# Attention probabilities reordered by key blocks before they go through HBM, and a new order of ScalarE's work in a stop

## The reference, cut to what matters

```python
for i in range(DEPTH):                      # DEPTH = 2, 1024 tokens, 1024 features, float32
    z = rmsnorm(h, norm1[i]) @ w_in[i]      # pool input, q, k, v
    ...
    attn_out = dilated_mixer(q, k, v)       # 12 heads of 64, three patterns (dilation 1, 4, 16)
    h = h + concat([pool_out, attn_out]) @ w_out[i]
    h = h + square(relu(rmsnorm(h, norm2[i]) @ w_up[i])) @ w_down[i]
    gate = sigmoid(rmsnorm(h, norm3[i]) @ w_gate[i])
    h = h + gate * (p[i] @ w_ple[i])
...                                         # then one hybrid layer of another kind

# dilated_window_attention, for one block of 128 queries of one head:
s = q_block @ keys_of_this_and_previous_block.T * 64 ** -0.5   # masked
e = exp(s - max(s))
o = (e / sum(e)) @ v                        # the kernel divides later, by shares of the patterns
```

## Time and profile before

| | |
|---|---|
| median of 3 runs | 3103.16 us (3102.33 to 3103.45) |
| the profiled execution | 3097.3 us, its span 3095.6 us |
| PE busy | 3005.9 us, 97% of the span |
| DVE, POOL, ACT busy | 2117.8, 1947.8, 1029.4 us |
| mean granted TensorE clock | 0.988 |

### The profile page before, as it was taken

The page is one execution under the profiler, slowest core; times in us unless marked ns, Lnnn a source line. Parts: engine busy times, 40 slices in busy tenths (PEclk is TensorE's granted clock), DMA queues, the critical chain, the costliest instruction groups (busy, mean ns, idle before and its releaser), DMA issues.

```text
span 3095.6 us, 39370 instructions
## 1 busy us (share of the span) xinstructions
PE 3005.9 (97%) x14012; PEld 2422.1 (78%) x14012; DVE 2117.8 (68%) x2868; ACT 1029.4 (33%) x1879; POOL 1947.8 (63%) x1630
## 2 busy tenths in 40 slices
PE   8899799999999999898999999999999999999999
PEld 7677588888888888666788888888888777788887
DVE  6666485556888965565485557888868988797223
ACT  4122144333444420221253334444331344402102
POOL 6632257887999646432358888999546544476575
PEclk9999899999999999999999999999999999999999
DMA  5666424446444322657334446554211100111112
GB/s 165 144 142 150 122 86 152 154 154 246 152 150 158 93 89 78 146 125 186 71 108 156 153 150 246 157 151 161 58 46 48 35 28 28 30 43 55 45 57 87
DMA packets 605969, 356.21 MB, mean 115 GB/s; under 512 B 300624, under 2 KB 534096, under 8 KB 604240
## 3 DMA queue, kind: packets, MB, share of 16 engines
q1 hardware_dynamic: 333216, 222.34, 23.7%
q10 hardware_dynamic: 272560, 131.37, 15.2%
HBM read 250.55 MB, written 99.94 MB: 113 GB/s over the span
## 4 chain that ended last, share of the span: by engine, by line
PE 82%; DVE 5%; DMA 4%; ACTq 4%; ACT 2%; issue 2%; SPq 0%; DVEq 0%
PE ring L1588 11%; PE ring L1590 11%; PE ring L1589 11%; PE ring L1834 4%; PE ring L1833 4%; PE ring L1832 4%; PE ring L1866 4%; PE ring L1865 4%; PE ring L1867 4%; ACTq L2260 3%; PE aux L1588 3%; PE aux L1590 3%; PE aux L1589 3%; DMA probs_scratch<-probs 3%; PE aux L1832 2%
## 5 line engine op out<-in xcount | busy, mean ns | idle before, releaser
L1295 POOL TENSOR_TENSOR w_hi<-w_raw,ones_r 128x512 fp32r<-128x512 f32 (+3 forms) x296 | 331.1, 1119 | 646.0 <-PE ring L1590 572.4
L1298 POOL TENSOR_TENSOR w_lo<-w_raw,w_hi 128x512 fp32r<-128x512 f32 (+3 forms) x296 | 376.8, 1273 | 23.2
L1588 PE MATMUL ring<-Q_hi,w_hi 128*128 128x512 f32 x752 | 300.3, 399 | 1.7 <-DVE Q_lo L2711 1.7
L1590 PE MATMUL ring<-Q_hi,w_lo 128*128 128x512 f32 x752 | 293.3, 390 | 0.0
L1589 PE MATMUL ring<-Q_lo,w_hi 128*128 128x512 f32 x752 | 293.0, 390 | 0.0
L1588 PE MATMUL ring<-P_hi,w_hi 128*128 128x512 f32 x656 | 268.3, 409 | 3.1 <-DVE v_feat L2784 1.8
L1589 PE MATMUL ring<-P_lo,w_hi 128*128 128x512 f32 x656 | 257.3, 392 | 0.0
L1590 PE MATMUL ring<-P_hi,w_lo 128*128 128x512 f32 x656 | 257.0, 392 | 0.0
L3215 DVE SCALAR_TENSOR_TENSOR conv_out<-conv_in,taps,conv_out 128x1021 f32<-128x1021 f32 (+29 forms) x120 | 187.9, 1613 | 0.2
L1588 PEld LDWEIGHTS ring<-Q_hi,w_hi 128*128 128x128 f32 x752 | 141.1, 188 | 56.4 <-issue 26.3
L1590 PEld LDWEIGHTS ring<-Q_hi,w_lo 128*128 128x128 f32 x752 | 141.2, 188 | 30.1
(11 more groups left out here) (488 smaller groups left out, 8496.3 us busy)
## 6 DMA issues: line engine op xcount, KB each, us to landing
hid_scratch<-stages SPq DMA_DIRECT2D x196, 256.0 KB, 2.1
w_raw<-in_w_in SPq DMA_DIRECT2D x84, 512.0 KB, 3.9
w_raw<-in_w_down SPq DMA_DIRECT2D x64, 512.0 KB, 3.6
p_slot<-hid_scratch ACTq DMA_DIRECT2D x50, 512.0 KB, 4.7
q_slot<-hid_scratch ACTq DMA_DIRECT2D x48, 512.0 KB, 4.7
probs_scratch<-probs ACTq DMA_DIRECT2D x40, 512.0 KB, 3.2
probs_t<-probs_scratch ACTq DMA_DIRECT2D x160, 128.0 KB, 3.0
w_raw<-in_w_up SPq DMA_DIRECT2D x36, 512.0 KB, 4.6
```

Source lines behind the costliest of these rows:

```text
L1295: g.tensor_tensor(w_hi[:, slot, ks], w_raw[:, slot, ks], one.broadcast_to([P, width, P]), ALU.mult).then_inc(w_hi_ready, 1)
L1298: g.tensor_tensor(w_lo[:, slot, ks], w_raw[:, slot, ks], w_hi[:, slot, ks].bitcast(F32), ALU.subtract).then_inc(w_ready, 1)
L1588: t.matmul(o, wh, xh, start=first, stop=False)
L1590: return t.matmul(o, wl, xh, start=False, stop=last)
```

## The change

`probs` is laid out by key groups first, so that what one load wants of a partition's row is one run of 256 numbers (1 KB). DVE's transposes write into that layout and `attend` reads from the same one, in runs of 32 numbers 1 KB apart. ACT's order in a stop becomes: loads of `fetch_probs`, exponentials, and `take_attended` last. `fetch_v` moves from ahead of the unit's first stop to behind its first `send_probs`. And `turn_p` and `take_p` of the second half of the tokens move behind the last `lower_h` and `raise_h`. In the diff below the loops of `fetch_probs` and `exp_block` in `attention_stop`, which stay as they are, are left out, and of `LATE` only DVE's side is shown; ACT's is alike.

```diff
-    probs = place("probs", [P, 2, 2, 256], at=at_Q + 14 * TILE)
+    probs = place("probs", [P, SQUARES, 2, 2, 2, 32], at=at_Q + 14 * TILE)
-    probs_t = place("probs_t", [P, 2, 2, 256], at=at_ple + 1024)
+    probs_t = place("probs_t", [P, SQUARES, 2, 2, 2, 32], at=at_ple + 1024)
...
                 mm = t.matmul(attend_bank[rows, cols], v_t[buf][:, jj, rows],
-                              probs_t[:, half, e, at + b * P:at + b * P + P], start=(b == 0), stop=(b == len(blocks) - 1))
+                              probs_t[:, :, half, e, at // P + b], start=(b == 0), stop=(b == len(blocks) - 1))
...
         def fetch_probs(l, unit, i):
             no = stops_before(l, unit, i)
             act.wait_ge(probs_sent, 16 * (no + 1))
             act.wait_ge(attended, step_no(l, unit, blocks_of(unit, i)[0]))
-            squares = probs_d[no % 2].rearrange("(a t) (x b j) -> b t x a j", a=SQUARES, b=SQUARES, j=32)
+            squares = probs_d[no % 2].rearrange("(a t) (b w) -> b t a w", a=SQUARES, b=SQUARES)
             for b in range(SQUARES):
-                to = probs_t[32 * b:32 * b + 32].rearrange("t x e k -> t (x e k)").rearrange("t (x a j) -> t x a j", a=SQUARES, j=32)
-                act.dma_start(to, squares[b]).then_inc(probs_back, 16)
+                act.dma_start(probs_t[32 * b:32 * b + 32].rearrange("t a x e k j -> t a (x e k j)"), squares[b]).then_inc(probs_back, 16)

         def attention_stop(l, parts):
-            for unit, i in parts:
-                if i >= 2:
-                    for j in blocks_of(unit, i - 2):
-                        take_attended(l, unit, j)
...
+            for unit, i in parts:
+                if i >= 2:
+                    for j in blocks_of(unit, i - 2):
+                        take_attended(l, unit, j)
...
                 elif kind == "step":
-                    if args[1] == 0:
-                        fetch_v(l, args[0])
                     attention_stop(l, unit_parts(*args))
                 elif kind == "send":
                     send_probs(l, *args)
+                    if args[1] == 0:
+                        fetch_v(l, args[0])
...
             for x in range(2):
-                mm = v.transpose(probs[:, x].rearrange("q e k -> q (e k)"), turned[x])
+                mm = v.transpose(probs[:, :, x].rearrange("q b e k j -> q (e k) b j"), turned[x].rearrange("q (n b j) -> q n b j", b=SQUARES, j=32))
...
-            if i in LATE:
+            if i in LATE and LATE[i][1] == 0:
                 turn_p(l, *LATE[i])
...
             lower_h(l, HN3_ORDER[-1:])
+            for c in range(2):
+                turn_p(l, c, 1)
```

More of the change, by code:

```diff
@@ L2249, in send_probs @@
             act.wait_ge(probs_turned, step_no(l, unit, blocks_of(unit, i)[-1]) + 1)
-            act.dma_start(probs_d[no % 2], probs[:].rearrange("q x e k -> q (x e k)")).then_inc(probs_sent, 16)
+            act.dma_start(probs_d[no % 2], probs[:].rearrange("q b x e k j -> q (b x e k j)")).then_inc(probs_sent, 16)
         def fetch_probs(l, unit, i):
@@ L2501, in _ @@
             for i in range(2 * UP - 1, 4 * UP):
-                if i in LATE:
-                    c, hf = LATE[i]
-                    woven(l, late_at(1 + 2 * hf, c))
+                if i in LATE and LATE[i][1] == 0:
+                    woven(l, late_at(1, LATE[i][0]))
                 raise_h(l, [HN3_ORDER[i]])
+            for c in range(2):
+                woven(l, late_at(3, c))
             for f in range(KC):
```

## The result

| | before | changed |
|---|---|---|
| median, runs on the same chip | 3102.74 us (4 runs, 3095.70 to 3103.45) | 3060.09 us (4 runs, 3056.16 to 3061.96) |
| ratio, 95% interval | 1 | 0.9866 (0.9848 to 0.9883) |
| the profiled execution | 3097.3 us | 3061.96 us, its span 3060.2 us |

The change makes the kernel 1.3% faster: some 41 us, where 61 had been worked out. The time lies in the range, 18 us above the forecast, but outside the 3028 to 3056 that the forecast mechanism was given for itself.

A forecast was written before the change was run, and what follows sets the result against it. PE, busy 97% of the span, bounds the kernel; waits of 23.4 + 20.3 + 1.7 = 45.4 us plus 16 of clock make 61.4 off 3097.3, 3035.9, and 5.9 to the median gives 3042 us; range 3018 to 3080.

The forecast's parts named there:

- the forecast mechanism: Attention of both layers: 45.4 us of PE idle and 16 of clock return, 3042 us; own range 3028 to 3056, chance 0.54.
- The issue by the lower bound: ACT's four probability loads per stop: issue of 706 ns a load nears 377 ns, gaining 1.3 us a stop.
- rival D: DVE's transposes and PE's attend: strided operands double both, 3086 us, with DVE's part perhaps 3095 to 3105; chance 0.05.
- the first term of the sum: PE's 39.7 us of waits for probability loads: 2 stay at layers' first loads, 14.3 in the tail, 23.4 go.
- the tail: Late attention stops: six waits for probabilities, 14.3 us, counted as kept; shorter issue's gain is taken by the copies' new wait.
- the crowded stop: Near 307 us, DMA engines busy: four issues of 11.6 us should come near 2.8; PE waits 13.1 us there.
- the question that the prediction left open: Crowded stop's 11.6 us of issue: up to 8.8 stays once a layer, or goes if small pieces each wait for large.
- The waits at new units: PE's waits at a unit's first stop, 6.3 us in one: moving fetch_v behind the first send_probs should end them.
- A: Attention: only new-unit waits go, the crowded stop's 13.1 us stay, clock returns 10 at most; 37 us gained, 3066; chance 0.24.
- B: Attention: more comes back, the tail loosens by 14 us and the clock returns 25; 84 us gained, 3019; chance 0.10.
- C: Every attention stop: attend waits for ACT's moved copies; at 2.5 us beyond the limit 3142 us, slower; chance 0.05.
- E: Attention: no change in time, if ACT's lateness is merely passed on to DVE's order; chance 0.02.

The follow-up runs named there:

- the reversal in both directions: Copies (take_attended) moved last alone on the kernel before: 3096.70 us, 0.9993; copies put back first on the changed kernel: 3063.39 us, 0.9890.
- the second profile of the changed kernel: The changed kernel measured once more with nothing altered: 3062.29 us, 0.9876 against the kernel before.
- the two mends together: Changed kernel with unit 3's fetch_v moved behind take_rows and the hx reloads spread over three panels: 3048.52 us, 0.9855 against the kernel before.

## Why the prediction was right or wrong

**What held.** The place: nearly all of the gain lies in the attention. The packets, to within 10. The issue by the lower bound: 706 to 453 ns, 1.0 us a stop where 1.3 was taken (the bound was 377 ns a load). The 20.3 us of `v_feat` and the 1.7 of `Q_lo` went. The clock gave back some 13 us for 16. Strided transposes and operands cost nothing: 716 ns for 717, and one matmul of `attend` has a median of 273 ns in both kernels. With that rival D is out. The quiet landing, 3.0 us, did not move.

**The step that failed** is the first term of the sum, "39.7 - 2 - 14.3 = 23.4 us go". The waits of `attend` fell by 8.1 us, to 31.6. By place, from the timeline (0.3 us are in stalls too small for it):

| | before | said to stay | measured |
|---|---|---|---|
| first load of a layer | 3.5 | 2 | 5.6 (2.02 and 3.58) |
| the other stops of units 0 to 4 | 21.9 | 0 | 5.6 (0.51; and behind a moved `fetch_v` 0.54, 2.63 and 1.96) |
| the tail, its stops in the crowd | 5.4 (0.27, 1.75 and 3.42) | 5.4 | 13.4 (4.50, 1.44 and 7.50) |
| the tail, the last two attends of a layer | 8.8 (4.21, 1.46 and 3.17) | 8.8 | 6.7 (1.29, 2.03, 1.80 and 1.57) |

The last two rows are the 14.3 us that were kept. Of the second layer's crowd before, two stalls:

```profile
1458.90 0.79 PE L1588 MATMUL ring<-pool_hi,w_hi 128*128 128x512 f32 x1 [5.43 <-DVE v_feat L2784]
...
1478.67 1.60 PE L1656 MATMUL aux<-probs_t,v_t 128*64 128x128 f32 x12 [3.42 <-DMA probs_t<-probs_scratch]
```

Three things were read wrongly in it.

*The crowd has more than one end.* The prediction took the crowded stop to be a matter of issue, and the issue did shrink: 11.56 us became 1.84 with the DMA engines as full as before. But the landings stayed long. The loads issued at 308 landed after 6.2 to 9.7 us (5.4 to 11.5 before), which is the wait of 4.50 us in the first layer. And `fetch_probs` begins only when the store has landed, and that store has 4 KB rows already; nothing in the change helps it. What the DMA engines did while it was under way, in the changed kernel from 1426 to 1442 us: the busy share in slices, and the issues.

```profile
DMA  9999999999999999999999999999999999679951
...
DMA packets 3805, 5.10 MB, mean 319 GB/s; under 512 B 1271, under 2 KB 2788, under 8 KB 3804
...
hx<-h_scratch SPq DMA_DIRECT2D x3, 512.0 KB, 12.4
probs_scratch<-probs ACTq DMA_DIRECT2D x1, 512.0 KB, 15.9
```

Six reloads of 512 KB are issued at 1424.5 on the other queue, the store at 1426.2. So what left under the name of `v_feat` came back in part under that of `attend`: at the two crowded places PE waited 13.1 + 5.4 us for `v_feat` and 5.4 for `attend`, 23.9 in all, and waits 13.4 now. That the reloads are the cause is borne out by the run that spreads them: no store took over 8.8 us in it.

For the question that the prediction left open: of the 11.56 us of crowded issue, up to 8.8 might have stayed; 1.84 us in all is measured, and 2.24 right behind the reloads with the pieces alone, so nearly all of it went with the number of pieces. The rule that the prediction cites from the Trainium skill (DMA: Bandwidth & Descriptors, "Queues, rings and completion order"), that a DMA engine changes between rings after a packet of descriptors, was taken there to keep the issue long; that was not so here. A store of 4 KB rows could still be slow to issue in the crowd (3.25 us with the pieces alone), and its landing was slow. What the engines did from piece to piece is not in the trace.

*A moved instruction stands in front of others.* `fetch_v` was held against the landing of the store and counted at 0 to 0.3 us. Behind the store its four issues take 3.3 to 6.3 us (889 ns a load at the median, for 705), not 2.95, so the cover of some 3 us is short; the first load of a layer is one that pays for it (5.6 us for 3.5). And the queue it was moved into was read only up to `fetch_probs`: for unit 3, `take_rows` comes next. That wait rose by 7.3 us, and putting it right brought it back to 5.3.

*The credit went to the wrong part.* The waits at new units were to end by moving `fetch_v`. The move alone gives 5 us; the pieces alone give all 41, and with them the new-unit wait at 142 fell from 6.3 to 1.7 us though `fetch_v` stays where it was. A microsecond less of issue in the stops before lets ScalarE come to the new unit earlier, and the issues right behind `fetch_v` are shorter too (1.4 us for 4.5). The prediction took 1.3 us a stop for the issue, but entered it in the sum only for the crowded stop and the tail: with the pieces alone, 23 of the 34 us between the profiled executions come in units 0 to 4.

Sum by the profiles: 8.1 + 20.3 + 1.7 for `attend`, `v_feat` and `Q_lo`, less 7.3 for `rows`, and 2.1 more gained at L2856 (the part of L1706), make 24.9 us of idle time where 45.4 were counted; with 13 of the clock 38, and 35.3 is measured between the profiled executions.

**The rivals.** A, in which the crowded stop stays, gave 3066 and was nearly right in time, but not in its reason: about half of the crowded stops' waiting stayed, by landings and not by issues. That the time came out inside the range is owed to the room that the range left for A. B's looser tail hardly came: its 14.3 us became 20.1, those of the last two attends 6.7 for 8.8. C, the moved copies: the wait exists, 7.5 us, in one crowded stop; but the reversal in both directions (0.9993 alone, 0.9890 for 0.9866 and 0.9876) shows no loss that can be told, and the second profile of the changed kernel has no such wait, so it is a new name for a late exponential. E is out.

**Still open.** Whether the two mends together are faster than the changed kernel. And the share of the crowded stops in the gain is read from single executions (6 of 34 us with the pieces alone, 14 to 16 of 31 to 35 in the changed kernel): no run changed the issue in quiet stops alone.

## What to carry to other kernels

An engine that issues loads and computes pays for the issue in its own stream. Where such an engine is the late one, multiply the issue time by the number of rounds before looking at landings: here 253 ns a load, four loads and 40 rounds come to 40 us, and the kernel with that part alone was as fast as the whole change. The product is an estimate, since the time comes back only where the engine is late. A reordering whose total is nothing can be a gain at one place and a loss at another, as that of `fetch_v` seems to be; comparing the kernels at fixed points of the program shows it. Before moving an instruction, list everything behind its new place up to the next wait of the bounding engine, and price it there, not where it came from. And after a change add up a wait under all its names; the releaser that the profile gives it can change while the time stays.

## What was not expected of the hardware

The duration of an issue goes with the shape of the pattern and not with the bytes: a load of 32 partitions in 1 KB pieces takes 453 ns, one of 16 partitions, half the bytes, 448 ns, and the old one in runs of 32 numbers 706 ns, for the same 128 KB; the store of 512 KB, in 4 KB rows, takes 344 ns. Half a load lands sooner, 2.4 us for 3.0.

With the DMA engines busy throughout, issues stretch: 11.6 us for four loads in small pieces (up to 6.4 us for one), 1.84 and 2.24 us for four with an eighth as many pieces. Few pieces are no safeguard, though: single stores of 128 rows of 4 KB took 3.7 us to issue in the kernel before and 3.25 us with the pieces alone, where 0.33 is usual. And `fetch_v`'s loads had a median of 705 ns in both kernels where they wait for their store to land, and of 826 to 889 ns in three where they stand right behind a store of 512 KB; four of them took up to 5.1 us there and 6.3 us here.
